# Latent attention with the values held still: two heads' turned probabilities move past them, split high and low, and the outputs arrive as columns

## The reference, cut to what matters

```python
def gqa_block(qblk, k, v):
    s = jnp.einsum('bqkgd,bskd->bkgqs', qblk, k, preferred_element_type=jnp.float32) * ATTN_SCALE
    p = jax.nn.softmax(s, axis=-1).astype(v.dtype)
    return jnp.einsum('bkgqs,bskd->bqkgd', p, v)
...
        if mixer == 0:
            q, k, v = qkv_proj(h, w_qkv[j], g_q[j], g_k[j])
            q = apply_axial_rope(q, cos, sin)
            ...
            y = latent_attention(q, k_all, v_all) @ w_o[j]
```

## Time and profile before

| | before |
|---|---|
| median of 3 runs | 3849.97 us (3849.85 to 3850.73) |
| profiled execution | 3849.88 us |
| its span | 3848.0 us |
| mean granted clock of TensorE | 0.942 |
| PE, weight loads, DVE, ACT, POOL busy | 91%, 80%, 58%, 44%, 35% |

### The profile page before, as it was taken

The page is one execution under the profiler, slowest core; times in us unless marked ns, Lnnn a source line. Parts: engine busy times, 40 slices in busy tenths (PEclk is TensorE's granted clock), DMA queues, the critical chain, the costliest instruction groups (busy, mean ns, idle before and its releaser), DMA issues. The chain is left out here.

```text
span 3848.0 us, 59509 instructions
## 1 busy us (share of the span) xinstructions
PE 3490.4 (91%) x19010; PEld 3071.8 (80%) x19010; DVE 2220.8 (58%) x4533; ACT 1680.2 (44%) x3971; POOL 1344.5 (35%) x1756
## 2 busy tenths in 40 slices
PE   5999979899999999797999848999998959999998
PEld 4899867899999988586888636888787748888786
DVE  5466766455677775436776256666435565666434
ACT  1277411667777770423333043333334463333333
POOL 2365332455666762311110324444101224444000
PEclk8999989999999989798999868999999769999999
DMA  3311346211222113300000021222354112222354
GB/s 151 118 40 40 134 183 234 77 44 42 62 61 64 55 59 153 128 1 6 0 0 18 26 104 67 86 82 82 115 180 155 53 49 77 82 84 85 126 194 145
DMA packets 97167, 333.01 MB, mean 87 GB/s; under 512 B 10673, under 2 KB 37601, under 8 KB 85090
## 3 DMA queue, kind: packets, MB, share of 16 engines
q1 hardware_dynamic: 96994, 330.90, 24.4%
HBM read 269.76 MB, written 61.10 MB: 86 GB/s over the span
## 5 line engine op out<-in xcount | busy, mean ns | idle before, releaser
L1964 PE MATMUL ps<-down_high,hidden_high 128*128 128x512 f32 x704 | 276.8, 393 | 15.1 <-DVE hidden_low L1865 14.7
L1947 PE MATMUL ps<-columns_combined,up_high_even 128*128 128x512 f32 x616 | 243.2, 395 | 46.1 <-POOL up_low_even L1732 32.7
L1965 PE MATMUL ps<-down_low,hidden_high 128*128 128x512 f32 x704 | 275.7, 392 | 0.0
L1966 PE MATMUL ps<-down_high,hidden_low 128*128 128x512 f32 x704 | 275.5, 391 | 0.0
L363 PE MATMUL ps<-w_hi,hT_hi 128*128 128x512 f32 x640 | 254.9, 398 | 21.3 <-ACTq L410 9.1
L1863 DVE TENSOR_TENSOR down_low<-down_raw,down_high 128x1024 fp32r<-128x1024 f32 x88 | 107.8, 1225 | 272.2 <-ACT down_high L1780 272.2
L364 PE MATMUL ps<-w_lo,hT_hi 128*128 128x512 f32 x640 | 253.8, 397 | 0.0
L365 PE MATMUL ps<-w_hi,hT_lo 128*128 128x512 f32 x640 | 253.5, 396 | 0.0
L1948 PE MATMUL ps<-columns_combined,up_high_even 128*128 128x512 f32 x616 | 242.5, 394 | 0.0
L1949 PE MATMUL ps<-columns_combined,up_low_even 128*128 128x512 f32 x616 | 242.5, 394 | 0.0
L1947 PE MATMUL ps<-columns_combined,up_high_odd 128*128 128x512 f32 x616 | 239.6, 389 | 0.0
(11 more groups left out here) (354 smaller groups left out, 9735.7 us busy)
## 6 DMA issues: line engine op xcount, KB each, us to landing
mod_weights<-in_w_mod SPq DMA_DIRECT2D x24, 2048.0 KB, 8.6
up_raw<-in_w_up SPq DMA_DIRECT2D x44, 1024.0 KB, 4.9
down_raw<-in_w_down SPq DMA_DIRECT2D x88, 512.0 KB, 3.7
hidden_columns<-hidden SPq DMA_DIRECT2D x44, 512.0 KB, 2.6
hidden_columns<-hidden_columns SPq DMA_DIRECT2D x88, 256.0 KB, 3.9
w_raw<-in_w_in_b SPq DMA_DIRECT2D x24, 768.0 KB, 4.4
group_rows<-unit_rows SPq DMA_DIRECT2D x64, 132.0 KB, 1.8
unit_rows<-group_rows SPq DMA_DIRECT2D x64, 132.0 KB, 2.1
```

Of the source, the lines that this page charges most:

```text
L1947: nc.tensor.matmul(out, a_hi, combined.moving(0, z, k), start=(start and k == 0), stop=False, **again)
L1964: nc.tensor.matmul(out, h_hi[:, s, t], down_hi[:, s, cols], start=begin, stop=False)
L1965: nc.tensor.matmul(out, h_hi[:, s, t], down_lo[:, s, cols], start=False, stop=False)
L1966: last = nc.tensor.matmul(out, h_lo[:, s, t], down_hi[:, s, cols], start=False, stop=end)
```

## The change

The values are split (ACT the high part, once, POOL the low part, in the place of the values themselves) and held in PE; the turned probabilities, split too, move. The three groups of each head are now all copied by ACT as high parts (`probsT_high`) and subtracted by DVE (`probsT_low`) for the low parts, and the scores of n+2 wait for DVE's subtraction of the same group. `out` works on pairs of heads: ten key tiles with three products 256 columns wide, the first five tiles at the even head behind, the others at the odd head. The result has head columns as partitions and queries as columns. So the division by the sums needs factors by column: DVE inverts the sums of two heads, ACT spreads them over 128 columns (`spread_sums`), PE turns them (`turn_factors`), ACT copies them (`take_factors`), and DVE multiplies (`out`) into X, which then holds columns. The scale of the next queries goes from DVE at head 2 to ACT at head 2, behind the exponentials of n+2, as eight instructions. The block that loads the gain is gone, its load is issued in the attention, as are the first loads and splits of `w_o`. The turn of outputs is gone; `project` gets `unsplit` columns, now also without `add`.

```diff
+            @block.sync
+            def _(sp):
+                sp.dma_start(gain, gain_dram.partition_broadcast(P)).then_inc(core.constants.sem, 16)
+                ahead.first_loads(sp)
...
-                            if part == 1:
-                                pe.wait_ge(core.probs_t_act.sem, core.probs_t_act.at(n - 1))
-                            else:
-                                pe.wait_ge(core.probs_t_dve.sem, core.probs_t_dve.at(2 * (n - 2) + 1 + part // 2))
+                            pe.wait_ge(core.probs_t_dve.sem, core.probs_t_dve.at(3 * (n - 2) + part + 1))
...
+                def turn_factors(p):
+
+                    pe.wait_ge(core.one_over.sem, core.one_over.at(p + 1))
+                    for x in range(2):
+                        last = nc.tensor.transpose(factor_bank[:, x * P:(x + 1) * P], spread[:, x], core.ident[:])
+                    return last
...
+                def out(pe, p, j, half):
+
+                    if half == 0:
+                        pe.wait_ge(core.probs_t_dve.sem, core.probs_t_dve.at(6 * p + 6))
+                        if isinstance(p, int) and p == 0:
+                            pe.wait_ge(core.values_low.sem, core.values_low.at(1))
+                        else:
+                            pe.wait_ge(core.heads_out.sem, core.heads_out.at(p))
+                    kv, s = 2 * j // rep, j % 2
+                    for kt in HALF_KEYS[half]:
+                        hi, lo = (x[:, kt, kv * HD2:(kv + 1) * HD2] for x in (v_hi, v_low))
+                        p_hi, p_lo = (x[:, s, kt].rearrange("p h t -> p (h t)") for x in (pT_hi, pT_lo))
+                        nc.tensor.matmul(o_bank, hi, p_hi, start=(kt == 0), stop=False)
+                        nc.tensor.matmul(o_bank, hi, p_lo, start=False, stop=False)
+                        last = nc.tensor.matmul(o_bank, lo, p_hi, start=False, stop=(kt == ALL_TILES - 1))
+                    if half == 1:
+                        last.then_inc(core.pv.sem, 1)
...
                 queries(0, first=True)
+                pool.wait_ge(core.values_high.sem, core.values_high.at(1))
+                pool.nop(nofuse=True)
+                pool.tensor_tensor(v_low[:], v, v_hi[:].bitcast(F32), ALU.subtract).then_inc(core.values_low.sem, 1)
                 with pool.Fori(1, TILES) as t:
                     queries(t)
+                ahead.first_splits(pool)
...
+                def query_scale(t):
+                    act.wait_ge(core.rstd.sem, core.rstd.at(t + 1))
+                    act.wait_ge(core.rot_pool.sem, core.rot_pool.at(2 * t))
+                    act.wait_ge(core.rot_dve.sem, core.rot_dve.at(3 * t))
+                    act.nop(nofuse=True)
+                    for h in range(QH2):
+                        last = act.activation(scaled[:, h * HD2:(h + 1) * HD2], q(t)[:, h * HD2:(h + 1) * HD2], ACT.Copy, scale=qrs[:, h:h + 1])
+                    last.then_inc(core.hidden.sem, 1)
+
+                def spread_sums(p, s):
+                    act.wait_ge(core.links_dve.sem, core.links_dve.at(p + 1))
+                    for x in range(2):
+                        last = act.activation(spread[:, x], core.ones[:], ACT.Copy, scale=rtotal[:, 2 * s + x:2 * s + x + 1])
+                    last.then_inc(core.one_over.sem, 1)
+
+                def take_factors(p):
+                    if not isinstance(p, int) or p > 0:
+                        act.wait_ge(core.heads_out.sem, core.heads_out.at(p))
+                    act.activation(factors[:], factor_bank, ACT.Copy).then_inc(core.parts_act.sem, 1)
+
                 def tile(act, t, first, more):
                     for h in range(QH2):
                         n = t * QH2 + h
-                        act.wait_ge(core.probs_t.sem, core.probs_t.at(3 * n + 2))
-                        act.activation(pT[:, h % 2, 4:8].rearrange("p k t -> p (k t)"), pt_bank(h % 2, 1), ACT.Copy)\
-                           .then_inc(core.probs_t_act.sem, 1)
+                        some = not (first and h < 2)
+                        for g in range(3):
+                            act.wait_ge(core.probs_t.sem, core.probs_t.at(3 * n + g + 1))
+                            if g == 0 and not (first and h < 4):
+
+                                act.wait_ge(core.pv.sem, core.pv.at(pair_of(t, h)))
+                            if g == 2 and some and h % 2 == 0:
+                                take_factors(pair_of(t, h))
+                            act.activation(pt(pT_hi, h, g), by_tiles(pt_bank(h % 2, g)), ACT.Copy).then_inc(core.probs_t_act.sem, 1)
+                        if h % 2:
+                            spread_sums(pair_of(t, h) + 1, (h // 2) % 2)
                         if more and h == QH2 - 2:
                             q_high(act, t + 1, 0)
                             q_high(act, t + 1, 1)
...
                             exps(act, n + 2, (h + 2) % QH2)
                         if more and h == 0:
                             query_squares(t + 1)
+                        if more and h == 2:
+                            query_scale(t + 1)
                 query_squares(0)
+                act.activation(v_hi[:], v, ACT.Copy).then_inc(core.values_high.sem, 1)
...
+                def one_over(p, s):
+                    dve.wait_ge(core.probs.sem, core.probs.at(2 * p + 2))
+                    dve.reciprocal(rtotal[:, 2 * s:2 * s + 2], total[:, 2 * s:2 * s + 2]).then_inc(core.links_dve.sem, 1)
+
+                def out(dve, p, t, j):
+                    dve.wait_ge(core.pv.sem, core.pv.at(p + 1))
+                    dve.wait_ge(core.parts_act.sem, core.parts_act.at(p + 1))
+                    dve.tensor_tensor(columns(t)[:, j * 2 * P:(j + 1) * 2 * P], o_bank, factors[:], ALU.mult).then_inc(core.heads_out.sem, 1)
 
                 def tile(dve, t, first, more):
                     for h in range(QH2):
-                        n = t * QH2 + h
-                        for g in (0, 2):
-                            dve.wait_ge(core.probs_t.sem, core.probs_t.at(3 * n + g + 1))
-                            k = GROUPS[g]
-                            dve.tensor_copy(pT[:, h % 2, k[0]:k[-1] + 1].rearrange("p k t -> p (k t)"), pt_bank(h % 2, g))\
+                        n, p = t * QH2 + h, pair_of(t, h)
+                        if h % 2:
+                            one_over(p + 1, (h // 2) % 2)
+                        for g in range(3):
+                            dve.wait_ge(core.probs_t_act.sem, core.probs_t_act.at(3 * n + g + 1))
+                            dve.tensor_tensor(pt(pT_lo, h, g), by_tiles(pt_bank(h % 2, g)), pt(pT_hi, h, g).bitcast(F32), ALU.subtract)\
                                .then_inc(core.probs_t_dve.sem, 1)
...
+            weights = Weights(core, st, I["w_o"])
             with ExitStack() as st2:
                 gain_q = core.sb(st2, "gain_queries", [P, D])
-                copies(core, [(gain_q[:], I["gain_q2"].partition_broadcast(P))])
-                latent_attention(core, tile_part(X)(0, D), gain_q[:], tables, kT_hi, kT_lo, v)
-        with ExitStack() as st:
+                latent_attention(core, x_rows(X), x_rows(X), gain_q[:], I["gain_q2"], tables, kT_hi, kT_lo, v[:], v_low, weights)
             T = split_columns(st)
-            weights = Weights(core, st, I["w_o"])
-            turn(core, TILES, Rows(core, tile_part(X)(0, D)), T, ahead=weights)
-            project(core, T, plain_tokens, TILES, weights, 2, lambda m, c: X[:, m, bass.ds(c * 512, 512)])
+            project(core, T, plain_tokens, TILES, weights, 2, lambda m, c: X[:, m, bass.ds(c * 512, 512)],
+                    unsplit=X[:].rearrange("p m (k t) -> p k m t", t=P))
```

More of the change, by code:

```diff
@@ L190, in __init__ @@
         self.gated = Count(nc, ctx, "gated")
+        self.values_high = Count(nc, ctx, "values_high")
+        self.values_low = Count(nc, ctx, "values_low")
+        self.one_over = Count(nc, ctx, "one_over")
     def mark(self):
@@ L295, in project, with like, split_high @@
     cw, w_hi, w_lo = weights.cw, weights.hi, weights.lo
+    def like(t, k):
+        return t[:, k].rearrange("p (m t) -> p m t", t=P) if len(unsplit.shape) == 4 else t[:, k]
+    def split_high(act):
+        for k in range(KT):
+            act.activation(like(t_hi, k), unsplit[:, k], ACT.Copy).then_inc(core.hi_done.sem, 1)
     with ExitStack() as st:
@@ L419, in _ @@
                     each_chunk(act, 0, taken)
-            if unsplit is not None:
-                assert add
+            if add and unsplit is not None:
                 @block.scalar
                 def _(act):
-                    for k in range(KT):
-                        act.activation(t_hi[:, k], unsplit[:, k], ACT.Copy).then_inc(core.hi_done.sem, 1)
+                    split_high(act)
     if side:
@@ L1376, in turn_probs @@
                                                        pr[:, h % 2, kt * P:(kt + 1) * P], core.ident[:])
+                        if g == 2 and factors_of is not None:
```

(25 more changed lines are left out.)

75 lines of the change are left out of this document (45 added, 30 removed).

## The result

| | before | after |
|---|---|---|
| median of 4 runs | 3849.91 us (3849.34 to 3850.73) | 3935.03 us (3927.45 to 3936.82) |
| profiled span | 3848.0 us | 3935.0 us |
| mean granted clock of TensorE | 0.942 | 0.939 |

The changed kernel is slower: ratio 1.0217, 95% interval 1.0199 to 1.0235, 85 us. Forecast were 3926 us, in a range of 3890 to 3990.

What follows compares the result with a forecast made beforehand. PE looked like the bound at 5.08 us a head, with an ACT/DVE path of 5.03 beside it. Loop +103.8, clock +7, tail +0.9, start -4.0, POOL +1, end -32.5: +76.2 on 3849.88, 3926 us, range 3890 to 3990.

Steps and rivals of the forecast that it cites:

- The forecast case: Whole kernel: the lengthened path through ACT and DVE sets the step, slower at 3926 us; chance 80%.
- The plain step: Between two heads of the attention loop: 6.38 us instead of 5.08, 1.30 more, with PE idle 1.5.
- the subtractions of groups 0 and 1 + 0.05 + 1.36: Path's end in each step: both DVE subtractions (1.30 us), then the restart of the scores, then the next `largest`.
- The heads with extras: Added per tile: head 1 +0.95 and +0.33, head 3 +0.33, head 4 +0.38, head 6 +2.1, scale +2.4; tile 57.5 us.
- list of signs: What the trace would show, such as `largest` to `largest` 6.4 us in plain heads and 8.8 in head 3.
- The clock: the mis-sized term: In the wait made by `query_scale`: one fall of PE's clock per tile, 1.0 us each, +7 (bounds 0 and 21).
- the term for POOL: At the attention's start: POOL's work beside DVE may stretch DVE's first heads, +1 us (0 to 3).
- Outside the loop: Before and after the attention loop: start -4.0 us, tail +0.9, end -32.5.
- Tail and end: Last pair without a next head: +0.9 us; last `out` to the projection, 3.2 instead of 35.75: -32.5.
- the rival in which PE stays the bound: Attention loop: subtractions not between copy and scores, step 4.85 us, total 3801; chance 5%.
- The rival of the engine with the highest share: The skill's rule to improve the engine with highest occupancy, TensorE; by it alone 3801 us, PE the bound, 5%.
- The clock that stays low: Attention loop: PE's clock, once down, might not get back, 4080 us, or about 4000 if half the time; together 12%.

Runs made afterwards that it cites:

- order_first: The changed kernel with ACT's high copies of head n written ahead of the exponentials of head n+1: 3788.64 us, ratio to before 0.9844.
- half_second: The changed kernel with only the subtraction of group 1 cut from 512 to 256 columns beyond the first four heads: 3930.1 us in one run, plain step 6.45.
- half_low: The changed kernel with the subtractions of groups 0 and 1 both cut from 512 to 256 columns beyond the first four heads: 3911.4 us in one run.
- fill_long: The changed kernel with unused extra PE products filling each wait to its measured length (8 to 26 at heads 0 to 6): 3919.79 us, ratio to before 1.0188.
- before_order: The kernel before the change, with ACT's copy of head n written ahead of the exponentials of head n+1: 3836.69 us, ratio 0.9967.

## Why the prediction was right, and where its working was not

The forecast case came in, 9 us above the 3926. By its own steps:

- **The plain step.** 6.38 forecast, 6.45 measured. The mechanism (high copies behind the exponentials, subtraction behind the copies) holds, by order_first. One part of its working was wrong: "the subtractions of groups 0 and 1 + 0.05 + 1.36". The second subtraction is not on the path (half_second), the scores' first part is, with 0.80 from start to start in its place: 0.75 + 0.80 + 1.26 are 2.81 by the starts; the forecast's two subtractions and what followed them were 2.71. I had carried the restart before part 1 over from rows 3, where part 0 had been free long before. The two errors nearly cancelled, and that was luck; a forecast for a smaller subtraction would have missed by half, as half_low's did.
- **The heads with extras.** Head 1: 7.66 forecast, 7.59. Head 3, behind the scale: 9.1 forecast in the working (8.8 in the list of signs, which left out DVE's 0.33), 8.98 undisturbed. Head 6: 8.48 forecast, 8.38. Head 4: 0.38 forecast, nothing measured: the two rotation products take 0.68 each and overlap by 0.08, 1.28 in all, which just fits between the subtractions' end at 1.54 and the scores' at 2.81; I had charged 0.94 + 0.61 for them. A tile at an undisturbed clock: 57.5 forecast, 57.2 in fill_long.
- **The clock: the mis-sized term.** "One fall per tile" and 7 us were forecast, with bounds 0 and 21. The tiles after are 62.13, 60.33, 59.93, 58.31, 59.22, 59.73 and 60.47 us, and the loop's clock 0.93. By step the excess over the undisturbed ones is 4.2 us at head 1 (four falls), 6.5 at head 3 (seven) and 6.5 at head 6 (six), 17.3 in all. A further 1.0 lies at the first head of the loop. fill_long got 15 us of it back. I had looked only at the longest wait; the row that I did not have was one for a wait of 2.5 us behind the waits of the neighbouring heads. The fall that the forecast did foresee, at head 3, cost 6.5 for its 7; what it lacked are the 10.7 at heads 1 and 6 and this 1.0. The loop grew by 122.1 where 103.8 + 7 were forecast, and the clock's 18.3 instead of 7 are as much as the whole difference (the tiles' 57.2 for 57.5 and the term for POOL, next, roughly cancel).
- **POOL beside DVE.** 1 us was forecast at the start; `values_low` cost nothing there, but the splits of `w_o` lengthened head 4 of the last full tile to 7.91, 1.5 us (the last section has the rows).
- **Outside the loop.** Start -4.0 forecast, -4.1 measured (without the 1.3 that had been gained earlier). `values_high` took 2.32 us (2.6 forecast) and `values_low` on POOL 5.63 (some 6), and nobody waited for either. Tail and end together -31.6 forecast, -31.7 measured. The last output ends at 2227.43 and the projection starts 2.97 later, with one high copy and one subtraction between, 3.2 forecast. The timeline of the kernel after, there:

```profile
2227.01 0.42 DVE L1610 TENSOR_TENSOR x<-ps,factors_by_query 128x256 f32<-128x256 f32 x1 [3.95 <-PE ps L1429]
...
2227.81 6.74 ACT L306 ACTIVATE hT_hi<-x 128x1024 fp32r<-128x1024 f32 x7 [4.16 <-PEq L1333]
...
2230.40 0.79 PE L374 MATMUL ps<-w_hi,hT_hi 128*128 128x512 f32 x1 [3.42 <-DVE hT_lo L398]
```

- **PE's own work.** 4.85 a head was forecast for the rival in which PE stays the bound; with the order changed the four plain steps of a tile average 4.76. The rival's 3801 us was near the time of a kernel that is one short edit away: order_first took 3789.
- **The rival of the engine with the highest share** fell for this kernel. The Trainium skill (Perfetto Trace Analysis, Identifying the Most-Contended Engine) would have one improve PE, which the change did; the traces show what that rule leaves out: a path 0.05 us shorter than PE's work was beside it, and it set the step once it had grown to 6.45. In the other order PE is the bound, and less work for it did shorten the loop (order_first against before_order, 14 us).
- **The clock that stays low** fell as a rival: it came back within each tile, though 17 falls were closer to it than the forecast had.

## What to carry to other kernels

When one engine looks full, add up the shortest round through all engines before making its work cheaper: follow one buffer from its release to its next release, with the queue positions in it. Here the split into high and low parts added two engines in series to such a round; it cost nothing once no other long instruction stood between the data and the copy, so write each engine's list in the order in which the data get ready. When two orders are possible, try the order together with the operations: the order alone gave 13 us, with the change 61, and what a moved operation costs (27 us or nothing, for the scale) is a property of the order.

## What the runs showed of the hardware

TensorE's granted clock fell from its upper level of 2.4 GHz to its lower one of 1.2 behind shorter waits than I had looked for. Three cases in the trace after, the first two at head 1 of two tiles:

```profile
1830.89 0.80 PE L1393 MATMUL ps<-kT_hi,qT_hi 128*128 128x512 f32 x1 [2.52 <-DVE probsT_low L1619]
...
2009.46 0.50 PE L1393 MATMUL ps<-kT_hi,qT_hi 128*128 128x512 f32 x1 [2.53 <-DVE probsT_low L1619]
...
2024.88 0.79 PE L1393 MATMUL ps<-kT_hi,qT_hi 128*128 128x512 f32 x1 [3.90 <-DVE probsT_low L1619]
```

Behind the idle 2.52 us at 1830.89 the first product took 0.80, the granted clock of 1831 to 1835 was 0.66, and the step took 8.69. Behind the idle 2.53 us at 2009.46 the first product took 0.50, and the step was the undisturbed 7.59. In four of the seven tiles this head took 8.47 to 8.95. Behind the idle 3.90 us at 2024.88 the first product took 0.79, and the granted clock of 2024.88 to 2029.00 was 0.59. Added products in the waits took nearly all falls away (0.99 in the loop), and those too many in the last tile cost 1.6 us. Why the same wait brings a fall in one tile and none in the next was not settled.

DVE beside POOL. The two rotation products of head 4 (both inputs in SBUF, 512 columns), in the kernel after, in the fifth tile and in the last full one:

```profile
2032.14 1.62 DVE L1619 TENSOR_TENSOR probsT_low<-ps,probsT_high 128x512 fp32r<-128x512 f32 x3 [1.97 <-ACT probsT_high L1540]
2033.67 0.68 DVE L1587 TENSOR_TENSOR rotation<-scaled_queries,axial 128x512 f32<-128x512 f32 x1
2034.27 0.68 DVE L1588 TENSOR_TENSOR rotation<-scaled_queries,axial 128x512 f32<-128x512 f32 x1
...
2150.57 1.62 DVE L1619 TENSOR_TENSOR probsT_low<-ps,probsT_high 128x512 fp32r<-128x512 f32 x3 [1.98 <-ACT probsT_high L1540]
2152.11 1.12 DVE L1587 TENSOR_TENSOR rotation<-scaled_queries,axial 128x512 f32<-128x512 f32 x1
2153.15 1.76 DVE L1588 TENSOR_TENSOR rotation<-scaled_queries,axial 128x512 f32<-128x512 f32 x1
```

In the second case POOL is splitting `w_o` (2150.08 on), in the first it has nothing to do. The products take 1.12 and 1.76 us instead of 0.68, and the head 7.91 instead of 6.46. The three subtractions ahead of them, with one input in PSUM, take 1.62 both times. So here work moved to POOL was free beside the subtractions and not beside operations on SBUF alone.

The Trainium skill (GPSIMD Engine Reference, Key points) says that POOL shares its SBUF interfaces with DVE, so that DVE's instructions with two SBUF inputs contend with it; these rows agree, and give the size, which it does not.
